# The first expert block of a transformer layer: its rows by selection products instead of a gather, bias rows added on chip, routing counts moved inside the block

## The chip, the cores and the metric

One core of a Trainium2 chip runs the whole program. Its engines are TensorE (PE, matrix products), VectorE (DVE), ScalarE (ACT), GpSimd (POOL) and SyncE (SP, whose queue only issues DMAs here). The metric is the device time of one execution in microseconds (us).

## The reference, cut to what matters

The kernel computes a whole layer: a retention branch and a differential attention branch, merged into `x_new` (512 tokens of 1024), then a mixture of 32 experts of which each token uses 4. The change touches only the passage into the experts and the first expert's block.

```python
def _moe(h, router_w, router_b, w1, b1, w2, b2):
    logits = (xt @ router_w + router_b).astype(jnp.float32)
    top_val, top_idx = lax.top_k(logits, TOP_K)          # TOP_K = 4 of N_EXPERTS = 32
    gate = jax.nn.softmax(top_val, axis=-1)
    ...                                                  # tokens sorted by expert, blocks of 128 rows
    def expert_block(args):
        xblk, e = args
        hh = xblk @ w1[e] + b1[e]
        glu = jnp.minimum(hh[:, :D_FF], SWIGLU_LIMIT)
        lin = jnp.clip(hh[:, D_FF:], -SWIGLU_LIMIT, SWIGLU_LIMIT)
        act = glu * jax.nn.sigmoid(SWIGLU_ALPHA * glu) * (lin + 1.0)
        return act @ w2[e] + b2[e]
    ...
    y = jax.ops.segment_sum(yb * row_gate[:, None], row_tok, num_segments=t + 1)[:t]
# _layer: x_new = x_new + g_f * _moe(_modulate(_rmsnorm(x_new, norm2_g), sh_f, sc_f), ...)
```

## The kernel before, in words

The order on each engine is written out by hand; semaphores tie the engines together. Each engine executes its own list in order, so an instruction that waits holds up all that stands behind it on that engine.

**Weights.** Every expert needs 12 chunks of 1 MB, eight of `exp_w1` and four of `exp_w2`. SP loads a chunk into one of six slots (`load_w1`, `load_w2`; a slot is free when DVE has used the chunk six before it, semaphore `e_lo`). ACT rounds it to a high part (`hi_e`, 1.92 us), DVE makes the low part (`lo_e`, 2.29 us), and PE multiplies three combinations (high by high, high by low, low by high), twelve matmuls of 512 columns for each chunk. Three of the six slots are not free at first: slot 3 holds rows 256 to 511 of the normalised tokens (`ht[2]`, `ht[3]`), slots 4 and 5 lie over the modulation vectors and `ht[0]`, `ht[1]`.

**Loop over experts.** `up(i)` on PE multiplies the block's 128 rows, transposed (`xthi`, `xtlo`), by the eight `exp_w1` chunks; `turn_x` transposes the rows of the next block out of the buffer that POOL's gather filled; `down(i-1)` multiplies by four `exp_w2` chunks; `turn_act(i)` transposes the activations. `item(i)` is these four in that order, 32 times (there is one extra block). Block 0 stands ahead of the loop: `up(0, bias_part)`, `turn_x`, `turn_act(0)`, and then the loop.

**Between the output projection and block 0** ("routing"). `out_part(t, c, kh)` on PE makes `x_new` of token tile t, half c. DVE adds the residual (`new_x`), ACT takes the sum of squares (`row_squares`), POOL the reciprocal root (`row_rstd`), DVE makes the rows (`scale_rows`, `shift_rows`; semaphore `n2_done`). PE transposes and multiplies by the router (`turn_rows`, `logits`; ACT copies between them, `x_columns`). DVE picks four experts (`choose(t)`, ending in the mask), PE counts places (`places(t)`), DVE computes gates and slots (`gates_of`, `place`) and, for experts 0 and 1, one-hot selection matrices (`pick_rows(t)`, tile `pick`). `first_rows(t)` multiplies those by token numbers, from which DVE makes the row lists of the first two blocks (`first_ready`). Then block 0 needs this chain: POOL gathers the 128 rows from `h2_d` in memory, SP loads the chunks 3 to 5 behind that gather, and PE does `turn_x`, ACT and DVE split the result (`x_high`, `x_low`). PE also makes counts over all tokens, flags and an item list (`route_step` 2 to 4) before block 0.

**POOL's list** writes every token's row number and gate into a table in memory (`list_tile(t)`: four indirect DMAs for each of four tiles, line 826), gathers, reads the table back (line 851), sets the next bias selector (`next_sel(0, 1)`, line 860), and adds the gated second biases into the output.

**Second bias.** PE forms gates times `b2` (`bias_part`, banks 6 and 7), ACT copies them out (`bias_out(t)`, four buffers), POOL scatter-adds each tile into `out` (line 896, four indirect DMAs of 512 KB), where SP has stored `x_new` before. Line 2089 is the helper `mm` for every matmul; lines 2504, 2605, 2616 and 2679 are transposes (of the token rows, of the gathered rows, of the activations, of the dense gates); 1231 is `hi_e`, 1913 is `lo_e`.

## Time and profile before

| | us |
|---|---|
| median of 3 runs | 2324.55 (2322.3 to 2326.19) |
| the profiled execution | 2324.45 |
| its span on the core | 2322.7 |
| PE busy in the span | 2275.3 (98%) |
| DVE busy | 1697.1 (73%) |
| ACT busy | 1222.1 (53%) |
| POOL busy | 377.7 (16%) |

The span is the time between the first and the last instruction of the core; some 2 us of the execution lie around it. A busy PE in these profiles is not PE at its peak: the granted clock (PEclk) says which of its two levels, 1.2 or 2.4 GHz, it ran at, 0.50 being 1.2 GHz. Times such as 1136.47 are microseconds from the span's start.

### The profile page before, as it was taken

The page shows a single profiled execution, that of the slowest core. Times are in us where ns is not written, and L with a number is a line of the kernel's source. Part 1 is how long each engine was busy: PE and PEld are TensorE (multiplying, and loading weights), DVE is VectorE, ACT ScalarE, POOL GpSimd, SP SyncE. Part 2 cuts the span into 40 slices and gives each one's busy share as a digit, 9 for nine tenths or more (in the row PEclk, how much of TensorE's full clock was granted, in tenths as well). Part 3 has the DMA queues.
Part 4 walks back from the last instruction along what each step waited for, and adds up shares of the span by engine and source line. Part 5 has one row for each costly group of instructions (what it writes and reads, how often), then busy time and mean ns, then how long its engine had stood idle before and what let it go on. Part 6 is the DMA issues. An engine that isn't in the chain of part 4 may idle for free.

```text
span 2322.7 us, 29938 instructions
## 1 busy us (share of the span) xinstructions
PE 2275.3 (98%) x10487; PEld 1802.7 (78%) x10487; DVE 1697.1 (73%) x1544; ACT 1222.1 (53%) x1136; POOL 377.7 (16%) x327
## 2 busy tenths in 40 slices
PE   7999999999999999999799999999999999999997
PEld 3858778686887787788678888888888888888886
DVE  4535344353636766856799999999999999999996
ACT  4212222121233723732577777777777777777774
POOL 2000000000203023000621212212211122121112
PEclk9999999999999999999799999999999999999999
DMA  8322313132231021054699999999999999999995
GB/s 294 118 91 91 127 37 128 54 123 77 73 111 52 1 91 55 1 168 161 238 378 385 370 370 379 368 375 373 374 364 371 363 370 378 367 373 376 369 372 180
DMA packets 135509, 542.89 MB, mean 234 GB/s; under 512 B 16131, under 2 KB 24467, under 8 KB 101390
## 3 DMA queue, kind: packets, MB, share of 16 engines
q1 hardware_dynamic: 123192, 516.30, 58.8%
q0 software_dynamic: 11952, 21.44, 3.8%
q10 hardware_dynamic: 296, 4.21, 0.5%
q8 instruction: 45, 0.74, 0.1%
q14 instruction: 24, 0.20, 0.0%
HBM read 533.79 MB, written 26.38 MB: 241 GB/s over the span
## 4 chain that ended last, share of the span: by engine, by line
PE 95%; DVE 1%; DMA 1%; ACT 1%; issue 0%; ACTq 0%; POOLq 0%; SPq 0%; DVEq 0%
PE ps L2089 91%; PE ps L2605 1%; PE ps L2616 1%; DMA raw<-in_w_mod 1%; PE ps L2407 1%; PE ps L2349 0%; DVE nmx L1696 0%; PE ps L2295 0%; DMA raw<-in_exp_w 0%; DMA ar<-h_d,ar 0%; ACT ar L1111 0%; PE ps L2425 0%; DVE hlo L1435 0%; PE ps L2504 0%; DVE ar L1431 0%
## 5 line engine op out<-in xcount | busy, mean ns | idle before, releaser
L2089 PE MATMUL ps<-whi,yhi 128*128 128x512 f32 x1072 | 348.5, 395 | 5.6 <-DVE yhi L2000 5.6
L2089 PE MATMUL ps<-hhi,yhi 128*128 128x512 f32 x1072 | 342.6, 389 | 0.0
L1913 DVE TENSOR_TENSOR hlo<-raw,hhi 128x2048 fp32r<-128x2048 f32 x132 | 302.4, 2292 | 48.5 <-ACT hhi L1231 48.5
L1231 ACT ACTIVATE whi<-raw 128x2048 fp32r<-128x2048 f32 x132 | 253.3, 1920 | 97.2 <-PE ps L2089 97.0
L1913 DVE TENSOR_TENSOR wlo<-raw,whi 128x2048 fp32r<-128x2048 f32 x132 | 298.8, 2284 | 4.9 <-ACT whi L1231 3.5
L1231 ACT ACTIVATE hhi<-raw 128x2048 fp32r<-128x2048 f32 x132 | 253.1, 1917 | 86.1 <-PE ps L2089 75.0
L1345 DVE TENSOR_TENSOR wlo<-raw,whi 128x2048 fp32r<-128x2048 f32 x56 | 128.2, 2289 | 219.3 <-ACT whi L929 219.3
L2089 PEld LDWEIGHTS ps<-whi,yhi 128*128 128x128 f32 x1072 | 202.6, 189 | 59.7 <-issue 12.1
L2089 PE MATMUL ps<-ar 128*128 128x128 f32 (+4 forms) x1014 | 237.5, 429 | 6.1 <-ACT ar L1145 1.4
L2089 PE MATMUL ps<-whi,hhi 128*128 128x512 f32 x592 | 233.7, 395 | 0.0
L2089 PEld LDWEIGHTS ps<-hhi,yhi 128*128 128x128 f32 x1072 | 201.2, 188 | 41.8
L2089 PE MATMUL ps<-whi,hlo 128*128 128x512 f32 x592 | 230.8, 390 | 0.0
L2089 PE MATMUL ps<-wlo,hhi 128*128 128x512 f32 x592 | 230.5, 389 | 0.0
L2089 PEld LDWEIGHTS ps<-ar 128*128 128x128 f32 (+1 forms) x1014 | 145.8, 192 | 92.5 <-issue 70.9
L929 ACT ACTIVATE whi<-raw 128x2048 fp32r<-128x2048 f32 x56 | 107.2, 1915 | 209.5 <-PE ps L2089 208.9
L2089 PE MATMUL ps<-wlo,yhi 128*128 128x512 f32 x544 | 213.1, 392 | 0.0
L2089 PE MATMUL ps<-hlo,yhi 128*128 128x512 f32 x544 | 211.7, 389 | 0.0
L2089 PE MATMUL ps<-whi,ylo 128*128 128x512 f32 x544 | 177.3, 395 | 1.9 <-DVE ylo L2019 1.9
L2089 PE MATMUL ps<-hhi,ylo 128*128 128x512 f32 x544 | 174.9, 390 | 0.6 <-DVE hlo L1913 0.5
L875 POOL DMA_INDIRECT out_x<-ar,cur x32 | 92.7, 2896 | 501.4 <-DVE ar L2029 468.8
L1913 DVE TENSOR_TENSOR wlo<-ar,whi 128x2048 fp32r<-128x2048 f32 x66 | 151.2, 2292 | 27.2 <-ACT whi L1231 27.1
L1231 ACT ACTIVATE whi<-ar 128x2048 fp32r<-128x2048 f32 x66 | 126.8, 1921 | 55.0 <-PE ps L2089 53.4
(293 smaller groups left out, 3962.8 us busy)
## 6 DMA issues: line engine op xcount, KB each, us to landing
raw<-in_exp_w SPq DMA_DIRECT2D x264, 1024.0 KB, 7.8
ar<-in_exp_w SPq DMA_DIRECT2D x132, 1024.0 KB, 7.7
raw<-in_w_in SPq DMA_DIRECT2D x44, 1024.0 KB, 5.0
raw<-in_w_mod SPq DMA_DIRECT2D x22, 1024.0 KB, 6.4
raw<-in_w_br_ret SPq DMA_DIRECT2D x8, 1024.0 KB, 5.1
ar<-in_x SPq DMA_DIRECT2D x8, 512.0 KB, 9.2
raw<-in_w_br_diff SPq DMA_DIRECT2D x4, 1024.0 KB, 5.2
raw<-in_w_out SPq DMA_DIRECT2D x4, 1024.0 KB, 10.2
```

The costliest lines, as they stand in the source:

```text
L875: pool.indirect_dma_start(a["out"], bass.IndirectOffsetOnAxis(ap=cur[:, 0:1], axis=0), F(A_Y, D), None, bounds_check=L - 1, oob_is_err=Fal ...
L929: act.activation(whi[:, j % NSPL, :, :], raw[:, s, :, :], ACT.Copy).then_inc(hi_made, 1)
L1231: act.activation(e_whi[j % ESPL], e_raw[s], ACT.Copy).then_inc(e_hi, 1)
L1345: V.tensor_tensor(wlo[:, j % NSPL, :, :], raw[:, s, :, :], whi[:, j % NSPL, :, :].bitcast(F32), ALU.subtract).then_inc(lo_made, 1)
L1913: V.tensor_tensor(e_wlo[j % ESPL], e_raw[s], e_whi[j % ESPL].bitcast(F32), ALU.subtract).then_inc(e_lo, 1)
L2089: return pe.matmul(out, lhsT, rhs, start=start, stop=stop, skip_group_check=skip)
L2407: last = pe.transpose(psf[:, TURN0 + m * P:TURN0 + (m + 1) * P], F(A_PROB, 2, 2, T)[:, u % 2, 0, m * P:(m + 1) * P], ident)
L2605: last = pe.transpose(ps[:, q, c * P:(c + 1) * P], F(A_XG, D)[:, k * P:(k + 1) * P], ident)
L2616: last = pe.transpose(ps[:, act_bank(i, hf), c * P:(c + 1) * P], F(A_AC, 2, COL)[:, hf, c * P:(c + 1) * P], ident)
```

## The change

It does the following.

1. Block 0's rows. `direct_rows(t, q)` on PE multiplies `ht[t]` by `pick[:, t, 0, :]`, 32 products of 128x128 in full precision, and so has the transposed rows of expert 0 in banks 0 and 1. The gather of block 0 goes; POOL's first gather is for expert 1, and `turn_x` for it moves into `up(0)` (after chunk 6).
2. Loads. SP loads chunk 4 as soon as the last row store is issued, chunk 5 when the stores have landed and `places(3)` is done, chunk 3 when the second `direct_rows` bank is done. None waits for a gather.
3. Routing counts, `first_rows`, flags, item list and the transposes of the gates are issued by PE after chunks 0, 1 and 2 of `up(0)` (`route(kk)`), and DVE's side of them, with `gates_of(3)` and `place(3)`, stands between `lo_e(0, 1)` and `lo_e(0, 4)`. The mask is no longer copied three times; one sum over the tiles (`mask_sums`) is.
4. The last tile's sum of squares is taken in two halves (`half_squares`), with one POOL addition more; `hi_e(0, 0)` to `hi_e(0, 2)` stand between ACT's steps of the last tile; `choose(3)` goes ahead of `shift_rows(3)`.
5. Second bias. `b2` is loaded three times, scaled by POOL (96x1024) instead of DVE, and the low part is made by POOL. `bias_part` comes one chunk later. ACT copies out into two buffers instead of four; POOL adds each tile to `x_new` on chip (`tensor_tensor` of 128x1024, `out_summed`) and stores it once. SP's four stores of `x_new` and the four scatter-adds go. `bias_out(2)` and `bias_out(3)` stand behind `glu(0)`.
6. After `up(0)` PE waits until ACT and DVE have read its banks, and starts `item(1)`; `turn_act(0)` is issued inside `up(1)`, after its chunk 1.

```diff
@@ SP
-            sp.wait_ge(first_ready, 1)
-            sp.wait_ge(gathered, 16)
-            for j in range(RSLOTS - 1, ERAW):
-                load_w1(0, 0, j)
-            for t in range(LT):
-                sp.dma_start(a["out"][t * P:(t + 1) * P, :], F(A_XN, LT, D)[:, t, :]).then_inc(stored, 16)
+            load_w1(0, 0, RSLOTS)
+            sp.wait_ge(h2_stored, 16 * LT)
+            sp.wait_ge(pos_done, LT)
+            load_w1(0, 0, RSLOTS + 1)
+            sp.wait_ge(xt_turned, 2)
+            load_w1(0, 0, RSLOTS - 1)
@@ POOL
             list_tile(1)
+            pool.wait_ge(b2_loaded, 48)
+            pool.wait_ge(vec2, 80)
+            hold()
+            pool.tensor_tensor(out=b2, in0=b2, in1=F(A_GFB, D)[0:3 * N_EXPERTS, :], op=ALU.mult).then_inc(b2_scaled, 1)
+            list_tile(2)
             pool.wait_ge(first_ready, 1)
             pool.wait_ge(h2_stored, 16 * LT)
-            gather(firsti[:, 0, 0:1])
-            list_tile(2)
+            gather(firsti[:, 1, 0:1])
+            pool.tensor_copy(cur[:, :], firsti[:, 0, :]).then_inc(cur_ready, 1)
+            pool.wait_ge(gb_hi, 1)
+            pool.tensor_tensor(out=b23[0:32, :], in0=b2[0:32, :], in1=b23[0:32, :].bitcast(F32), op=ALU.subtract).then_inc(gb_lo, 1)
             list_tile(3)
...
             next_sel(0, 1)
-            pool.wait_ge(stored, 16 * LT)
             for t in range(LT):
+                if t == LT - 1:
+                    next_gather(0, 2)
                 pool.wait_ge(gb_out, 2 * t + 2)
                 hold()
-                pool.indirect_dma_start(a["out"], bass.IndirectOffsetOnAxis(ap=lval[:, t * TOP_K, 0:1], axis=0),
...
+                pool.tensor_tensor(out=xn, in0=xn, in1=bias_rows[t % 2], op=ALU.add).then_inc(out_summed, 1)
+                pool.wait_ge(out_summed, t + 1)
+                pool.dma_start(a["out"][t * P:(t + 1) * P, :], xn).then_inc(stored, 16)
@@ ACT
             def bias_out(t):
...
+                if t >= 2:
+                    act.wait_ge(out_summed, t - 1)
...
+            for j in range(ESPL + 1, FIRST):
                 hi_e(0, j)
             bias_out(0)
+            hi_e(1, 0)
+            bias_out(1)
+            hi_e(1, 1)
+            x_high(1, (0,))
             act.activation(junk32[:, 0:1], ones[:, 0:1], ACT.Silu)
             glu(0)
+            x_high(1, (1,))
+            bias_out(2)
+            bias_out(3)
@@ DVE
             x_low(0)
+            lo_e(0, 1)
+            gates_of(3)
+            place(3)
+            dve.wait_ge(route_step, 1)
...                                      # flag, then
+            lo_e(0, 2)
+            dve.wait_ge(route_step, 2)
...                                      # lists of the first blocks, flags, then
+            lo_e(0, 3)
...                                      # bias low parts, item list, then
+            lo_e(0, 4)
@@ PE
+            def direct_rows(t, q):
+                pe.wait_ge(pick_ready, t + 1)
+                pe.wait_ge(n2_done, t + 1)
+                for c in range(4):
+                    k = 4 * q + c
+                    last = mm(ps[:, q, c * P:(c + 1) * P], ht[t][:, k * P:(k + 1) * P], pick[:, t, 0, :],
+                              t == 0 and c == 0, t == LT - 1 and c == 3, True)
+                if t == LT - 1:
+                    last.then_inc(xt_turned, 1)
...
+            pe.wait_ge(route_ready, 1)
+            direct_rows(0, 0)
             logits(3, 1)
+            direct_rows(0, 1)
+            direct_rows(1, 0)
+            direct_rows(1, 1)
             places(3)
+            for t in range(2, LT):
+                for q in range(2):
+                    direct_rows(t, q)
...
-            up(0, bias_part)
-            pe.wait_ge(gathered, 32)
-            turn_x()
-            turn_act(0)
-            pe.wait_ge(xt_lo, 4)
+            up(0, first_block)
+            pe.wait_ge(glu_done, 1)
+            pe.wait_ge(moe_step, 1)
+            pe.wait_ge(xt_lo, 3)
...
+            item(1, first_act)
```

## Rows read from the trace of the kernel before

**Rows 1.** Busy time by stage: from:to, length, then each engine's us, PEclk, DMA share, GB/s
```profile
1110.00:1120.00 10.00, 7.89 (x45) 7.12 (x43) 8.42 (x31) 3.35 (x7) 4.95 (x7) 0.76 0.20 68
1120.00:1130.00 10.00, 5.18 (x31) 4.46 (x31) 7.51 (x26) 6.55 (x6) 7.10 (x6) 0.50 0.20 46
1130.00:1140.00 10.00, 4.38 (x13) 3.26 (x12) 4.28 (x4) 6.04 (x7) 8.32 (x8) 0.50 0.97 361
1140.00:1150.00 10.00, 10.00 (x40) 8.14 (x39) 9.91 (x8) 5.76 (x3) 3.18 (x2) 0.87 1.04 394
...
1300.00:2322.00 1022.00, 1009.80 (x4687) 828.99 (x4685) 938.76 (x545) 731.43 (x484) 195.41 (x147) 1.00 0.96 361
```

**Rows 2.** The chain of waits from 1123 to 1192 us: start, us, what
```profile
1123.79 4.21 DMA ar<-h_d,ar
...
1128.12 5.09 DMA raw<-in_exp_w
...
1136.47 27.78 PE ps L2089 x108
...
1168.40 22.71 PE ps L2089 x100
```

**Rows 3.** PE in order of time: start, us, instruction, count, idle before and releaser
```profile
1137.06 0.63 PE L2089 MATMUL ps<-wlo,yhi 128*128 128x512 f32 x1
...
1138.34 0.63 PE L2089 MATMUL ps<-wlo,yhi 128*128 128x512 f32 x1
...
1143.04 0.39 PE L2089 MATMUL ps<-wlo,yhi 128*128 128x512 f32 x1
...
1143.72 0.39 PE L2089 MATMUL ps<-wlo,yhi 128*128 128x512 f32 x1
...
1166.92 1.09 PE L2616 MATMUL ps<-cst,ar 128*128 128x128 f32 x8 [1.81 <-DVE ar L2013]
```

**Rows 4.** PE in order of time, 799 us: full-precision products of 128x128, two instructions each
```profile
799.04 1.60 PE L2089 MATMUL ps<-ar 128*128 128x128 f32 x12
```

**Rows 5.** DVE in order of time, from the last tile into block 0
```profile
1113.05 0.69 DVE L1812 TENSOR_TENSOR ar<-ar,cst 128x512 f32<-128x512 f32 x1
...
1116.00 1.30 DVE L1824 SCALAR_TENSOR_TENSOR raw<-raw,rs,ar 128x1024 f32<-128x1024 f32 x1 [0.94 <-POOL rs L774]
1117.42 0.25 DVE L1842 SCALAR_TENSOR_TENSOR ar<-ps,rs,ar 128x32 f32<-128x32 f32 x1
...
1118.76 0.38 DVE L1857 TENSOR_REDUCE ar<-ar 128x32 f32<-128x128 f32 x1
...
1124.32 2.29 DVE L1913 TENSOR_TENSOR wlo<-raw,whi 128x2048 fp32r<-128x2048 f32 x1
...
1139.13 4.49 DVE L1913 TENSOR_TENSOR hlo<-raw,hhi 128x2048 fp32r<-128x2048 f32 x2
```

**Rows 6.** ACT in order of time: the first copy of the second bias out of PSUM
```profile
1150.96 1.09 ACT L1307 ACTIVATE ar<-ps 128x512 f32<-128x512 f32 x2 [1.08 <-PE ps L2089]
```

**Rows 7.** POOL in order of time, 1125 to 1154 us
```profile
1125.14 2.36 POOL L826 DMA_INDIRECT list_d<-ar  x1 [0.30 <-issue]
...
1136.06 0.96 POOL L826 DMA_INDIRECT list_d<-ar  x1 [0.30 <-issue]
...
1142.97 0.83 POOL L851 DMA_DIRECT2D ar<-list_d  x1 [0.62 <-DMA list_d<-ar]
1152.61 1.17 POOL L860 CAST hhi<-cst 128x128 fp32r<-128x128 f32 x1 [8.82 <-issue]
```

**Rows 8.** Line 851, POOL's read of the list table: issue to landing
```profile
DMA to landing us min/median/max: 8.3/8.3/8.3
```

**Rows 9.** DMA issues, 1090 to 1180 us: the load of 128 KB in the quiet stretch
```profile
ar<-in_exp_b SPq DMA_DIRECT2D x1, 128.0 KB, 3.9
```

**Rows 10.** Line 1624, a DVE product of 128x512: min, median and max ns
```profile
L1624 DVE TENSOR_TENSOR ar<-ar,rs x20: 693/1448/1454, 604.4 to 908.0; 128x512 f32<-128x512 f32 x20
```

**Rows 11.** Line 797, POOL's product of 128x512: min, median and max ns
```profile
L797 POOL TENSOR_TENSOR ar<-ar x20: 1032/1037/2082, 599.1 to 903.1; 128x512 f32<-128x512 f32 x20
```

More of the change, by code:

```diff
@@ L500, in build @@
         onehot = R(LT * TOP_K, N_EXPERTS)
-        mask3 = R(LT, 3 * N_EXPERTS)
+        mask = R(LT, N_EXPERTS)
+        mask_sums = R(3, N_EXPERTS)
         slot = R(LT * TOP_K)
@@ L1234, in _, with x_high @@
             acthi = ylo[:, 0:2, :].rearrange("p a (k n) -> p (a k) n", n=P)
-            def x_high(n):
-                for q in range(2):
+            def x_high(n, halves=(0, 1)):
+                for q in halves:
                     act.wait_ge(xt_turned, n * 2 + q + 1)
@@ L1995, in _, with x_low @@
             actlo = ylo[:, 2:4, :].rearrange("p a (k n) -> p (a k) n", n=P)
-            def x_low(n):
-                for q in range(2):
+            def x_low(n, halves=(0, 1)):
+                for q in halves:
                     dve.wait_ge(xt_hi, n * 2 + q + 1)
@@ L2045, in _ @@
             x_low(0)
-            for j in range(1, KH):
-                lo_e(0, j)
+            lo_e(0, 1)
+            gates_of(3)
+            place(3)
+            dve.wait_ge(route_step, 1)
+            V.tensor_scalar(small[0:96, 0:1], ps[0:96, 0, 0:1], cst[0:96, C_THR:C_THR + 1], None,
+                            ALU.is_gt).then_inc(flag_ready, 1)
+            lo_e(0, 2)
+            dve.wait_ge(route_step, 2)
+            firsti = first[:, :, :].bitcast(I32)
+            tl.did(V.tensor_scalar(pad[:, 2:4], ps[:, 1, 0:8:4], pad[:, 1:2], pad[:, 0:1], ALU.mult, ALU.add))
+            tl.did(V.tensor_copy(first[:, 0, 1:2], ps[:, 1, 2:3]))
+            tl.did(V.tensor_copy(first[:, 1, 1:2], ps[:, 1, 7:8]))
+            tl.wait()
+            V.tensor_tensor(firsti[:, :, 0:1], pad[:, 2:4].unsqueeze(2), ps[:, 1, 1:8:4].unsqueeze(2),
+                            ALU.add).then_inc(first_ready, 1)
+            dve.wait_ge(route_step, 3)
+            tl.did(V.tensor_copy(small[0:96, 1:2], ps[0:96, 0, 0:1]))
+            tl.wait()
+            dve.wait_ge(flag_ready, 1)
+            V.tensor_scalar(small[0:96, 8:8 + OVER + 2], iota[0:96, 0:OVER + 2], small[0:96, 1:2], small[0:96, 0:1],
+                            ALU.is_equal, ALU.mult).then_inc(flag_ready, 1)
+            lo_e(0, 3)
             dve.wait_ge(ones_made, 5)
@@ L2609, in turn_act @@
                 pe.wait_ge(act_done, i + 1)
-                if isinstance(i, int):
+                early = isinstance(i, int) and i == 0
+                if early:
                     pe.wait_ge(gb_out, 2 * LT)
                 for hf in range(2):
-                    if not isinstance(i, int):
+                    if not early:
                         pe.wait_ge(xt_lo, i * 2 + 3 + hf)
@@ L2622, in up @@
                 pe.wait_ge(e_lo, chunk(i, 0) + 1)
-                late = isinstance(i, int)
+                late = isinstance(i, int) and i == 0
                 def add_bias():
@@ L2666, in down, with item @@
                     last.then_inc(e_used, 1)
-            def item(i):
-                up(i)
-                pe.wait_ge(gathered, i * 16 + 32)
+            def item(i, between=None):
+                up(i, between)
+                pe.wait_ge(gathered, i * 16 + 16)
                 pe.wait_ge(act_lo, i * 2)
@@ L2674, in item, with first_block @@
                 turn_act(i)
-            pe.wait_ge(route_ready, LT)
-            pe.wait_ge(dense_ready, LT)
-            for t in range(LT):
-                last = pe.transpose(ps[0:N_EXPERTS, 7, t * P:(t + 1) * P], dense[:, t, 2:2 + N_EXPERTS], ident)
-            last.then_inc(route_step, 1)
-            pe.wait_ge(first_ready, 1)
-            pe.wait_ge(items_ready, 1)
-            pe.wait_ge(gathered, 16)
-            turn_x()
-            pe.wait_ge(xt_lo, 1)
-            def bias_part(kk):
-                t = kk - 3
+            pe.wait_ge(route_ready, LT - 1)
+            pe.wait_ge(xt_lo, 1)
+            def first_block(kk):
+                if kk < 3:
+                    route(kk)
+                if kk == FIRST - 2:
+                    pe.wait_ge(items_ready, 1)
+                    pe.wait_ge(first_ready, 1)
+                    pe.wait_ge(gathered, 16)
+                    turn_x()
+                t = kk - 4
                 if not 0 <= t < LT:
```

198 lines of the change are left out of this document (90 added, 108 removed).

## The prediction, made before the changed kernel was seen to run

> **What bounds the kernel now.** I read the busy time by stage first. From 1300 us to the end PE is busy 1009.8 of 1022 us at full clock, DVE 939 and the DMA engines 0.96 [rows 1]: in the expert loop PE is the bound, and nothing that the change does there shortens it. The hole is ahead of it: from 1110 to 1140 PE works 17.5 us of 30 and the granted clock falls to 0.50, the 1.2 GHz level, where it stays until past 1140. Then the chain of waits through the hole: the gather of block 0's rows takes 4.21 us, the load of chunk 3 that stands behind it 5.09 us, and PE starts block 0 at 1136.47; it has done `up(0)` at 1164.25 and starts the loop at 1168.40 [rows 2]. After that the chain is PE alone, 35.3 us for each block. So the change is worth what it moves the point at which PE gets through `up(1)`, less the work that it puts on PE on the way. The third view is each engine in order of time, since the new order has to be followed.
>
> **Start of block 0.** `new_x` of the last half tile ended at 1113.74 [rows 5]; without two mask copies and with `scale_rows` ahead of `choose(2)` it ends some 0.6 us sooner. The halved squares save about 0.4 us and the added POOL addition, one more small step there, costs back about 0.3 (all three are estimates). `choose(3)` no longer stands behind `shift_rows(3)`: it starts when its logits are there, about 1115.7 instead of 1117.42, and its mask takes 1.7 us as now (1117.42 to 1119.14) [rows 5], 1117.5. Then the sum over the mask, `shift_rows(3)` (1.3) [rows 5] and `pick_rows(3)` (0.7): the last selection matrix stands at 1119.9. PE has 32 selection products; twelve instructions, that is six products of this size, took 1.60 us including one drain of 0.28 [rows 4], so 0.24 to 0.27 each, taken as 0.25; 28 of them lie behind the last logits, 7.0 us, with 0.4 for `places(3)`: the last bank is done at 1122.9, the first 1.0 earlier. One copy on ACT (0.57) and one subtraction on DVE (0.7) give block 0 its start at 1123.3, against 1136.47: 13.2 us. This is the mechanism that the change is built on, and I believe it. These products keep PE working in full array passes where it idled, so I take the clock as full here; were it at 1.2 GHz, the 28 products would take twice as long, 7 us more.
>
> **Inside block 0.** Chunks cost PE 12 matmuls of 0.227 us (0.68 for three) at full clock and 0.427 at half (1.28 for three) [rows 3]. In block 0 about 14 ran at half clock, so `up(0)` at full clock is 27.78 - 14 x 0.2 = 24.9 us. The change adds `route(0)` to `route(2)`, some 26 small products and four transposes at 0.11 us per instruction, 3.2 us, and `turn_x` of 0.9 us. It also adds waits, since DVE gives only 2.21 us per low part (4.49 for two) [rows 5] and now does `gates_of(3)` and `place(3)` (2.3 us), lists and flags (1.3), bias low parts (1.4) and the item list (0.8) between them. Walking DVE through: `lo_e(0, 2)` ends at 1132.3 where PE wants it at 1130.9 (1.4 us), `lo_e(0, 4)` at 1141.9 where PE wants it at 1139.1 (2.9 us, of which 2.0 are POOL's, below). With these the last product of `up(0)` is at 1156.1, before it was 1164.25: 8.1 of the 13.2 us are left.
>
> **POOL and DVE exclude one another.** POOL's product of 128x512 takes 1.03 us [rows 11]. The DVE product at line 1624 takes 0.69 us alone and 1.45 when POOL's falls on it [rows 10]. The other way round, an indirect DMA issue of POOL takes 0.96 us beside an idle DVE and 2.36 at 1125.14, when the low part of 1124.32 ran; it ended 0.9 us after that [rows 5, 7]; the selector copy at 1152.61 took 1.17 for 0.29 in the same way. So where DVE makes low parts back to back, POOL gets one issue done for each of them, 2.2 us instead of 0.96 + 0.30. And the 96x1024 and 128x1024 operations that move to POOL (six of them) are priced at 2 x 1.03 = 2.07 us each for POOL and at up to as much for DVE. The Trainium skill (SBUF - State Buffer, "SBUF: two separate sides") says that this port pair is an exclusive lock, held for the whole instruction, and that a DVE operation with two SBUF inputs takes it too. By that rule each of the four additions costs DVE its full 2.07 us; the row at line 1624 shows 0.76 of 1.03 lost, by which it would be 1.5.
>
> **What is late next: POOL's list.** In the new order the loop cannot start before POOL has (a) read the list back and made the selector of block 1 (`next_sel(0, 1)`), and (b) added tile 0, because `bias_part(3)` on PE waits for `bias_out(2)`, and that for `out_summed` 1. Queued behind that wait are, on ACT, `hi_e(1, 2)` and all later high parts, on PE the whole loop. Before, line 860 ran at 1152.61 [rows 7], 16 us ahead of the loop. POOL's list of work, each step at its own duration and held by DVE as above: `list_tile(1)` ends at 1123.1; scaling `b2` 2.07, 1125.2; `list_tile(2)` among `lo_e(0, 1)` to `lo_e(0, 3)`, 1134.5; gather and `cur` 1137.5; low part of `b2` 2.07, 1139.6; `list_tile(3)` among `lo_e(0, 4)` to `lo_e(0, 7)`, four issues at 2.2 to 3.0 us, 1150.3 (1141.8 if DVE never holds it). Then the table writes land: 3.2 us after the issue, as the gather's 4.21 less its 1.05 of issue [rows 2] (5.9 us in the full queues before, from 1137.0 to 1142.9). The read-back of 128 KB took 8.3 us in full queues [rows 8]; a load of that size in a quiet stretch took 3.9 [rows 9]. The queues are fuller than quiet and emptier than before (SP's 2 MB of stores at 1129 to 1132, with loads issued right behind them, are gone, but loads still follow each low part), so I take 4.3: 1157.8. Register loads and the selector 1.3, as from 1151.3 to 1152.6; the addition 2.07, 1161.3; `bias_out(2)` 1.09 [rows 6]; `bias_part(3)` 0.5. The loop starts at 1163, before at 1168.40. That is 5.4 us.
> The Trainium skill (SBUF - State Buffer, "The DMA setup-cost knee") gives a fixed cost of about 2 us for any transfer; taken for both landings this is an estimate of 1159.7 for the loop's start and of 2320 for the time. The landings above are longer wherever the trace has one.
>
> **Behind the start.** PE has then stood for over 6 us. In the trace it came out of such a stretch at half clock for 6 us, 14 matmuls at 0.2 us more [rows 1, 3]: 2.9 us. `turn_act(0)`, 0.87 us, is now inside `up(1)`. Its old wait for the activation (1.81 us) [rows 3] is gone, and that is in the start already. The other POOL additions fall on DVE's low parts of block 1, but PE at half clock leaves DVE room: nothing. The loads hide: chunk 4 is issued at 1119 where the first was at 1128.1, and chunk 3, issued at 1123, has landed by 1130, ahead of `hi_e(0, 3)`'s use. The end of the kernel stays as it is.
>
> **The sum.** 5.4 - 0.9 - 2.9 = 1.6 us off the profiled execution of 2324.45, which stands 0.1 us from the median: 2323.0.
>
> **The rivals.** (1) *The list is on time.* If POOL's issues slip in between DVE's operations, `list_tile(3)` ends at 1142 to 1145, and the additions are ahead of need. Then the loop starts 3.3 us behind `up(0)` (`glu(0)` 1.0, `x_high` 0.55, `bias_out(2)` 1.1, `bias_part(3)` 0.5): 1159.4, 9.0 us early. Less 0.9 for `turn_act(0)`, and less 1.4 for a low part of block 1 that an addition delays: 6.7 us, 2317.8. No clock is lost. For it: many issues in the trace did take 0.96. Against it: those fell where DVE idled. (2) *Slower: the list is later still.* If landings are as in the trace of before (5.9 and 8.3 us) and the addition waits for one low part (2.2), the loop starts at 1172, 3.6 us late; with 0.9 and 2.9 on top 7.4 us slower: 2331.9. Place: line 851's landing. The price turns into a loss once the loop starts later than 1164.6. For it: those are the only durations that the trace has of these two transfers. Against it: the queues had just been given 2 MB of stores then. (3) *Block 0 starts late*, at half clock (7 us more) or because `shift_rows(3)` comes after `choose(3)`. POOL's list hides most of this: some 3 us more than the forecast, 2326. That the gather leaves the chain is not in doubt; a variant in which the change gives nothing for lack of effect has no chance of its own.
>
> **How the numbers follow.** The forecast 0.45 (2320 to 2326), rival 1 0.30 (2314 to 2320), rival 2 0.17 (2328 to 2334), rival 3 0.08. A measurement can tell about 0.2% here, 4.65 us: faster means below 2319.9, slower above 2329.2. Faster takes rival 1 and a little of the forecast's edge, 0.34; slower most of rival 2 and a little of rival 3, 0.18; within, 0.48. The range leaves out the far half of rival 2 and the far edge of rival 1: 2315.5 to 2330.5. The likeliest case alone has 2320 to 2326.
>
> **What would show it.** In the profile after: PE's first 512-column matmul of block 0 near 1123 (right) or past 1127 (the selection products or the clock); clock 1.00 from 1110 to 1155; line 1913's low part 4 ending near 1142; POOL's `list_tile(3)` issues near 2.2 us each and ending near 1150 (rival 1: 1.3 and 1144); the read-back landing near 1158; the loop's start near 1163 with PE idle 6 us ahead of it and at half clock behind it. Wrong is the prediction if PE is not idle there (rival 1), or if the loop starts past 1165 (rival 2).

## The result and the profile after

The kernel after takes 2326.91 us in the median (2323.67 to 2330.49), the kernel before 2323.42 beside it (2321.79 to 2326.19): ratio 1.0014, 95% interval [1.0008, 1.0021]. It is 3.5 us slower, where 1.6 us faster was forecast; the time lies inside the range. The profiled execution took 2326.59 us with a span of 2324.8.

The same stages as in [rows 1], then the chain of waits as in [rows 2] (start, us, what) and PE's own waits (us in total, times, longest):

```profile
1110.00:1120.00 10.00, 8.47 (x74) 8.17 (x73) 8.08 (x22) 6.02 (x10) 6.40 (x9) 1.00 0.30 97
1120.00:1130.00 10.00, 8.22 (x37) 7.39 (x37) 8.29 (x10) 2.14 (x3) 8.86 (x5) 0.66 0.91 311
1130.00:1140.00 10.00, 10.00 (x59) 8.20 (x59) 9.21 (x22) 5.85 (x5) 4.42 (x2) 1.00 0.98 353
1140.00:1150.00 10.00, 8.87 (x39) 6.41 (x38) 9.94 (x5) 8.08 (x8) 9.22 (x5) 1.00 0.80 288
1150.00:1160.00 10.00, 6.20 (x32) 4.86 (x30) 6.54 (x7) 5.88 (x7) 3.76 (x3) 0.91 0.84 322
1160.00:1170.00 10.00, 3.40 (x9) 1.92 (x10) 1.80 (x1) 2.36 (x5) 6.59 (x6) 0.50 0.49 172
```
```profile
1135.57 3.90 POOL ar L835
1139.49 1.77 POOL cur L855
1141.26 2.38 POOL ylo L858
...
1151.34 7.09 DMA list_d<-ar
1158.43 0.29 issue
1158.71 2.67 DMA ar<-list_d
...
1163.06 2.31 POOL ar L908
1165.41 0.04 issue
1165.46 1.09 ACT ar L1325 x2
1166.55 0.04 issue
1166.60 9.46 PE ps L2098 x30
```
```profile
PE ps L2098 <- ACT ar L1325: 10.4, 1, 10.4
PE ps L2098 <- DVE ar L1911: 3.1, 1, 3.1
PE ps L2098 <- DVE wlo L1931: 1.1, 2, 0.7
```

The hole of [rows 1] at 1110 to 1140 is gone: PE works 26.7 of 30 us there. It has moved to 1150 to 1170, where PE works 9.6 of 20 us; from 1160 on the granted clock is at 0.50, the 1.2 GHz level. The second view names what ends last there: POOL's list of work (gather, `cur`, low part of `b2`, `list_tile(3)`), the landing of the list, its read-back, the first addition, `bias_out(2)`. That is the chain of the forecast. In the third view PE waits 10.4 us for `bias_out(2)` and 3.1 us for `pick_rows(3)`.

The profiles differ ahead of the change as well, so times of the passage are counted from an anchor that all kernels share, the start of the eight transposes of `turn_rows(1)` (1091.27 before, 1089.53 after). From the end of `up(1)` to the last transposes of the loop every profile has 1106.1 us, so a kernel's span is the sum of the anchor, the column "`up(1)` done", 1106.1 and the last column. The columns between are start times counted from the anchor. E-numbers are the experiments; e5, e10 to e13 and e15 are told in the text.

| kernel | anchor | block 0 starts | last product of `up(0)` | loop starts | `up(1)` done | last transposes to the end |
|---|---|---|---|---|---|---|
| before | 1091.27 | 45.20 | 72.57 | 77.13 | 99.68 | 25.68 |
| after | 1089.53 | 35.79 | 66.28 | 78.21 | 103.58 | 25.60 |
| after, second profile (e9) | 1089.57 | 31.54 | 66.11 | 76.77 | 102.86 | 28.38 |
| e1 | 1090.47 | 31.54 | 66.85 | 70.48 | 96.40 | 28.26 |
| e2 | 1091.02 | 31.54 | 67.05 | 72.16 | 99.04 | 26.98 |
| e3 | 1090.97 | 31.54 | 65.88 | 76.71 | 101.96 | 27.28 |
| e4 | 1089.38 | 31.54 | 66.48 | 73.21 | 99.61 | 28.14 |
| e6 | 1089.68 | 31.54 | 66.03 | 72.43 | 97.31 | 26.94 |
| e7 | 1089.47 | 31.54 | 70.68 | 74.31 | 99.00 | 26.96 |
| e8 | 1090.85 | 31.54 | 62.14 | 65.99 | 95.07 | 26.91 |
| e16 | 1089.74 | 31.54 | 67.65 | 71.77 | 98.08 | 25.60 |
| e17 | 1089.75 | 31.54 | 66.80 | 75.29 | 101.64 | 25.63 |
| e14 | 1089.13 | 31.54 | 63.68 | 67.48 | 96.53 | 25.97 |
| e18 | 1089.55 | 31.54 | 62.10 | 65.73 | 91.63 | 25.95 |

Block 0 starts 9.4 us sooner than before, the last product of `up(0)` comes 6.3 sooner, and the loop starts 1.1 us later; `up(1)` is done 3.9 us later. The anchor gave 1.7 back in this profile, so the span is 2.1 longer.

In this profile one more thing shows: DVE and POOL collide. The rows are DVE with `pick_rows(3)` at line 1911, then POOL with a list issue at line 831 and the scaling of `b2` at line 849, then PE before and behind its wait:

```profile
1118.39 3.33 DVE L1911 TENSOR_SCALAR ar<-ar 128x128 f32<-128x128 f32 x2
```
```profile
1118.30 0.96 POOL L831 DMA_INDIRECT list_d<-ar  x1 [0.30 <-issue]
1119.29 2.35 POOL L849 TENSOR_TENSOR ar<-ar 96x1024 f32<-96x1024 f32 x1
1121.81 2.99 POOL L831 DMA_INDIRECT list_d<-ar  x1 [0.17 <-issue]
...
1135.57 3.90 POOL L835 DMA_INDIRECT ar<-h_d,ar  x1 [5.62 <-DVE ar L2042]
```
```profile
1116.69 2.03 PE L2098 MATMUL ps<-ar,raw 128*128 128x128 f32 x16
1121.78 3.78 PE L2098 MATMUL ps<-ar,raw 128*128 128x128 f32 x16 [3.06 <-DVE ar L1911]
```

`pick_rows(3)` takes 0.48 us in every other profile of these kernels and 3.33 here: it ends at 1121.72, when POOL has ended both the issue and the scaling (1121.64). It also began 1.1 us later from the anchor than in e9, behind a wait for PE of 1.03 us whose reason stays open. PE stands 3.06 us, falls to the lower level, and makes the last 16 products in 3.78 us instead of 2.03 (at full clock 0.13 each, as in [rows 4]). Less the 0.57 us that PE stands ahead of block 0 in e9, this is the difference between 31.54 and 35.79 in the table.

### The profile page after: what moved, and what is told of

Same layout as the page of the kernel before. It is cut to its first block, busy times and chain, and to the rows that moved or that the text cites. A ratio compares the mean times of both kernels' runs of the same rounds, so it can differ in the third digit from the quotient of the medians.

```text
span 2324.8 us, 30027 instructions
## 1 busy us (share of the span) xinstructions
PE 2278.1 (98%) x10537; PEld 1805.2 (78%) x10537; DVE 1698.8 (73%) x1535; ACT 1221.6 (53%) x1137; POOL 370.8 (16%) x333
## 4 chain that ended last, share of the span: by engine, by line
PE 95%; DVE 1%; POOL 1%; DMA 1%; ACT 1%; issue 1%; POOLq 0%; DVEq 0%; SPq 0%; ACTq 0%
PE ps L2098 91%; PE ps L2651 1%; PE ps L2639 1%; PE ps L2416 1%; PE ps L2358 0%; DMA raw<-in_w_mod 0%; DMA list_d<-ar 0%; DVE nmx L1713 0%; PE ps L2304 0%; POOL list_d L831 0%; ACT ar L956 0%; POOL ar L835 0%; PE ps L2513 0%; ACT ar L1122 0%; PE ps L2434 0%
## 5 line engine op out<-in xcount | busy, mean ns | idle before, releaser
L2098 PE MATMUL ps<-ar 128*128 128x128 f32 (+5 forms) x1046 | 239.0, 422 | 3.0 <-ACT ar L1156 1.4
L885 POOL DMA_INDIRECT out_x<-ar,cur x32 | 86.5, 2704 | 508.7 <-DVE ar L2012 476.0
L1931 DVE TENSOR_TENSOR hlo<-ar,hhi 128x2048 fp32r<-128x2048 f32 x66 | 148.3, 2287 | 10.8 <-ACT hhi L1248 10.8
```

The costliest lines, as they stand in the source:

```text
L885: pool.indirect_dma_start(a["out"], bass.IndirectOffsetOnAxis(ap=cur[:, 0:1], axis=0), F(A_Y, D), None, bounds_check=L - 1, oob_is_err=Fal ...
L1931: V.tensor_tensor(e_wlo[j % ESPL], e_raw[s], e_whi[j % ESPL].bitcast(F32), ALU.subtract).then_inc(e_lo, 1)
L2098: return pe.matmul(out, lhsT, rhs, start=start, stop=stop, skip_group_check=skip)
```

## The experiments

Medians stand beside those of the kernel before on the same chip.

**Who holds the loop's start.** e1 moves POOL's additions of tiles 0 and 1, with `next_sel(0, 1)`, ahead of the wait for the list; e2 only the selector; e3 puts four powers of 128x8 (7.45 us on POOL, results unused) behind `list_tile(3)`; e4 puts the scaling of `b2` behind `list_tile(2)`.

```diff
# e1
+            next_sel(0, 1)
+            for t in range(2):
+                add_tile(t)
             pool.wait_ge(listed, 16 * LT * TOP_K)
...
-            next_sel(0, 1)
-            for t in range(LT):
+            for t in range(2, LT):
# e3
             list_tile(3)
+            for k in range(4):
+                hold()
+                pool.tensor_tensor(out=idle_t[:, 8 * k:8 * k + 8], in0=ones[:, 0:8], in1=ones[:, 8:16], op=ALU.pow)
```

> The changed kernel with POOL's order altered: the selector of block 1 and the additions of tiles 0 and 1 stand ahead of the wait for the list and of its read-back. Theory (POOL's list and read-back hold up the loop, through bias_out(2) and bias_part(3)): PE's stand of 10.4 us ahead of the last bias_part shrinks to about 3 us, the loop starts some 7.5 us sooner, and if the clock then holds another 2 us come back: ratio to the kernel before 0.998 (about 2319; 2317 with the clock), against 1.0014 for the changed kernel. Rival (DVE, held by POOL's operations, is what is late in block 0 and block 1): the additions only move DVE's losses elsewhere, ratio stays within 0.001 of 1.0014.

> The changed kernel with only the selector of block 1 ahead of the wait for the list; the additions stay behind the read-back. Theory: no change in time (ratio 1.0014 within 0.0007), PE's stand stays near 10 us, since the addition of tile 0 is the later of the two. If the selector alone were what the loop waits for, the time would fall by up to 4 us.

> The changed kernel with four small POOL operations (128x8 powers, 2.08 us each in the trace of before) put behind list_tile(3); they write a scratch tile that nobody reads. Theory: POOL's list is on the path, so the whole delay, some 8 us, or about 5 where it runs while the list writes are landing (5.5 us between the last write and the read-back), shows: the wait for the landing covers up to 5.5 us of it, so 3 to 8 us slower than the changed kernel. Rival (POOL is off the path): no change.

> The changed kernel with POOL's scaling of b2 moved behind list_tile(2), so that it doesn't fall on DVE's pick_rows(3). Theory: pick_rows(3) takes 0.5 us instead of 3.3, PE doesn't stand 3.1 us ahead of the last selection products and the clock doesn't fall there (1.8 us), block 0 starts 4 us sooner, first_ready comes 2 to 4 us sooner, and with it POOL's list and the loop: 2 to 4 us faster than the changed kernel, ratio 0.9997 to 1.0006. Rival (POOL's list is late for its own length and not for first_ready): no change in time, though block 0 starts sooner.

Before 2323.67. e1 2322.32, ratio 0.9991 [0.9982, 1.0]; e2 2325.84, 1.0010 [1.0001, 1.0019]; e3 2328.31, 1.0016 [1.0007, 1.0025]; e4 2324.86, 1.0005 [0.9996, 1.0014]. PE's waits in e1:

```profile
PE ps L2103 <- DVE wlo L1936: 4.9, 3, 3.1
PE ps L2103 <- ACT ar L1330: 2.6, 1, 2.6
PE ps L2103 <- DVE hlo L1936: 2.1, 2, 1.4
```

With two additions ahead of the wait for the list the wait for `bias_out(2)` falls from 10.4 to 2.6 us (9.1 in e9, the second profile of the kernel after) and the loop starts at 70.5: the addition behind the list is the link. The time fell by 4.6 us and not by the nearly 8 expected; PE now waits 7.0 us for low parts, where it is 4.4 in e9.

e2's median stayed where it was expected, but its profile did not: PE waits 4.1 us for `bias_out(2)`, not near 10, and the loop starts 4.6 us sooner than in e9. The addition is still behind the read-back. About 2 us of the difference are in the addition, which took 2.34 us in e2 and 4.37 in e9, beside a low part of DVE. The medians of the two (2325.84 and 2325.69) do not show it at all, so e2 does not settle what the selector alone costs.

e3 was expected 3 to 8 us slower than the kernel after; its ratio is the same within the intervals (1.0016 and 1.0014). In the profile its 7.45 us moved the loop by nothing against e9 (76.71 and 76.77): 4.7 of them fell into the time in which POOL had waited for the list's landing anyway, and the rest was made up in the read-back (3.8 us to the selector in e3, 5.5 in e9) and in the addition (2.33 us in e3, 4.37 in e9). So this experiment does not price a delay of POOL; it shows the landing's wait as slack for POOL, not for the chain.

e4 takes the scaling out of the way of `pick_rows(3)`. It holds `hi_e(0, 3)`, which stands on ACT behind the copy of the scaled rows (it started after 10.51 us of waiting), and PE waits 5.0 us there, so `up(0)` ends no sooner than in e9. But POOL's list ended 3.0 us sooner than in e9 and the loop started 3.6 sooner. The ratio is within the range that was expected.

**The same delay in the kernel before, and parts undone.** e5 is the kernel before with e3's four powers. e6 is the kernel after with the scatter-adds, SP's stores of `x_new` and the four bias buffers back. e7 is the kernel after with `list_tile(3)` ahead of the wait for `first_ready`.

```diff
# e6
+            for t in range(LT):
+                sp.dma_start(a["out"][t * P:(t + 1) * P, :], F(A_XN, LT, D)[:, t, :]).then_inc(stored, 16)
...
-                pool.tensor_tensor(out=xn, in0=xn, in1=bias_rows[t % 2], op=ALU.add).then_inc(out_summed, 1)
...
+                pool.indirect_dma_start(a["out"], bass.IndirectOffsetOnAxis(ap=lval[:, t * TOP_K, 0:1], axis=0),
# e7
             list_tile(2)
+            list_tile(3)
             pool.wait_ge(first_ready, 1)
```

> The kernel before with the same four small powers on POOL behind `list_tile(3)`, 7.45 us of POOL time, that the kernel after was given. Theory (POOL's list became the last link only through the change): in the trace of before line 860 ran 16 us ahead of the loop, so 7.45 us vanish in that slack: 2323.4, within 1 us of the kernel before, and PE's row of waits as in [rows 2]. Rival (any 7 us of POOL work in this stretch cost, through DVE or through the loop's own POOL steps): 2326 or more.

> The kernel after with its selection products and routing inside block 0, but with the second-bias rows stored as before: four stores of x by SP, four scatter-adds by POOL, four bias buffers. `bias_out(2)` then waits for no addition. Theory (the wait of `bias_out(2)` for POOL's addition is what held the loop's start): the loop starts 3 to 5 us behind the last product of `up(0)`, 71 to 73 us after the anchor where it was at 78.2; with the 2 MB of stores in the queues some 1 to 2 us go back to late chunks: 2320 to 2323. Rival (the start and the clock of block 0 are what cost): still 2326 to 2327.

> The kernel after with `list_tile(3)` ahead of POOL's wait for `first_ready` (the gather of block 1's rows, `cur` and the low part of `b2` come behind it). Theory (POOL stood 5.6 us idle in the middle of its list and that time is on the path): the list's writes, the read-back and the first addition come 4 to 5 us sooner, the loop starts at 73 to 75 after the anchor, time 2323 to 2324.5. Rival 1 (the idle time is hidden, since the list's landing is paced by DVE's low parts): 2326 to 2327. Rival 2 (the gather for block 1 now becomes late for `turn_x`): PE shows a wait for the gathered rows inside block 0 of 2 us or more, and the time is 2326 or above.

Before 2323.52. e5 2324.39, 1.0001 [0.9992, 1.001]: in the kernel before the list is off the path; the powers took 10.46 us there, held by DVE, and cost nothing that can be measured. e6 2323.76, 1.0002 [0.9993, 1.0011]: the loop starts at 72.4 instead of 76.8 to 78.2, and 2 to 3 us come back in the median (against 2325.69 of e9 and 2326.91). That is a little short of the 2320 to 2323 expected: without the additions on chip the change is even with the kernel before, not faster. e7 2324.58, 1.0003 [0.9994, 1.0012], with both of its mechanisms at once:

```profile
PE ps L2098 <- POOL ylo L859: 6.1, 1, 6.1
PE ps L2098 <- ACT ar L1325: 2.6, 1, 2.6
```

The wait for `bias_out(2)` is down to 2.6 us, so the end of `list_tile(3)` was on the path. It does not show that the 5.62 us were, in which POOL stood idle in the first profile: without the collision they are gone from the kernel after too (in e9 POOL stands 0.30 us ahead of its gather). What e7 takes out from ahead of `list_tile(3)` is the gather, `cur` and the low part of `b2`, 5.8 us in e9. And now PE waits 6.1 us inside block 0, not for the gathered rows, as the second rival had it, but for POOL's low part of `b2`, which stands behind the same four issues.

**Improving on it.** e8 is e1 with chunk 3 loaded ahead of chunk 5 and with both products of the second bias on DVE; e16 has the first of the two alone (in the diff, what follows the loads is e8's, on DVE; the two POOL products go).

```diff
             sp.wait_ge(pos_done, LT)
-            load_w1(0, 0, RSLOTS + 1)
             sp.wait_ge(xt_turned, 2)
             load_w1(0, 0, RSLOTS - 1)
+            load_w1(0, 0, RSLOTS + 1)
...
             lo_e(0, 1)
...
+            V.tensor_tensor(b2, b2, F(A_GFB, D)[0:3 * N_EXPERTS, :], ALU.mult).then_inc(b2_scaled, 1)
...
             lo_e(0, 3)
...
+            V.tensor_tensor(b23[0:32, :], b2[0:32, :], b23[0:32, :].bitcast(F32), ALU.subtract).then_inc(gb_lo, 1)
```

> The order of the additions of e1 (two tiles ahead of the wait for the list), and two further moves: SP issues chunk 3's load ahead of chunk 5's, and the two products of the second bias (scaling and low part) are made by DVE, 1.22 us each, behind `lo_e(0, 1)` and `lo_e(0, 3)`, and no longer by POOL at 2.4 us each with DVE held. Theory (in e1 PE's 4.9 us of waits inside block 0 come from chunk 3's late landing and from POOL's product lying on DVE's bias rows): those waits fall to 2 to 3 us, 2319.5 to 2320.5. Rival (the waits inside block 0 are absorbed by the waits ahead of the loop): 2322.3 as e1.

> e1 with chunk 3's load issued ahead of chunk 5's and nothing else; the two products of the second bias stay on POOL. Theory (both parts of e8 carry: chunk 3's landing, and POOL's products lying on DVE): half of the 2.7 us between e1 and e8, 2320.5 to 2321.5. Rival 1 (the landing is all): 2319.7. Rival 2 (POOL's products are all): 2322.3.

e8: 2319.65 beside 2323.52, 0.9975 [0.9964, 0.9986]. e16: 2322.43 beside 2323.93, 0.9995 [0.9985, 1.0004], no better than e1 (0.9991). The landing alone brings nothing, since the next wait takes its place; PE's first row of waits in e16:

```profile
PE ps L2103 <- POOL ylo L858: 3.8, 1, 3.8
```

POOL's low part took 2.4 us plus what DVE held it; on DVE it took 1.21, and `bias_lo` beside it 1.40 instead of the 3.56 that e1 had. The last product of `up(0)` comes at 62.1 instead of 66.9. e16's median is that of its second rival, but no run has the DVE products without the load, so how the 2.7 us between e1 and e8 divide stays open.

**The end of the kernel.** In most profiles of kernels with the changed PE program the last column of the table is 1.2 to 2.7 us longer. From the last transposes to the first product of the last `down` (kernel before, kernel after, e9):

```profile
2297.02 1.03 PE L2616 MATMUL ps<-cst,ar 128*128 128x128 f32 x8
2299.95 0.49 PE L2089 MATMUL ps<-whi,ylo 128*128 128x512 f32 x1 [1.90 <-DVE ylo L2019]
```
```profile
2299.20 1.03 PE L2651 MATMUL ps<-cst,ar 128*128 128x128 f32 x8
2303.21 0.49 PE L2098 MATMUL ps<-whi,ylo 128*128 128x512 f32 x1 [2.98 <-issue]
```
```profile
2298.52 1.03 PE L2651 MATMUL ps<-cst,ar 128*128 128x128 f32 x8
2302.75 0.79 PE L2098 MATMUL ps<-whi,ylo 128*128 128x512 f32 x1 [3.19 <-issue]
```

Before, PE waits until DVE has the operand, 2.93 us in all (2.98 in e5, with the same PE program). After, it stands 4.01 and 4.23 us and the profile shows nothing that it waits for ("issue"); between the two lie only the jumps past the blocks that are not needed. In e9 the clock then falls, which it did not in the first profile (columns as in [rows 1]):

```profile
2300.52:2302.52 2.00, 0.00 (x0) 0.00 (x0) 1.02 (x3) 2.00 (x2) 1.59 (x1) 0.84 0.04 8
2302.52:2304.52 2.00, 1.77 (x4) 1.49 (x5) 2.00 (x2) 1.31 (x1) 0.00 (x0) 0.50 0.42 41
2304.52:2306.52 2.00, 2.00 (x6) 1.52 (x6) 2.00 (x1) 0.00 (x0) 0.00 (x0) 0.50 0.36 70
```

In the first profile of the kernel after the longer stand cost nothing. In the kernel before PE waits once more inside this `down`, for the low part of its last chunk; in the kernel after it comes there later and finds it made. The chains of waits, before and after:

```profile
2302.91 2.30 DVE hlo L1913
2305.21 0.04 issue
2305.25 7.11 PE ps L2089 x30
```
```profile
2301.91 1.30 issue
2303.21 11.34 PE ps L2098 x48
```

From the last transposes to the end of these products are 15.34 and 15.35 us. In e9, with the clock down behind the stand, they are 18.19.

e9 is the kernel after unchanged. e10, e11 and e12 are e8 with 64, 128 and 192 more PE instructions (waits that always hold) in the part that is jumped over. e13 is the kernel before with 200 more of them at the start of its PE program, as many as the change added; e14 and e15 are e8 with 56 and 128 more at the start. The diff is e14's; two such waits make one instruction.

```diff
             pe.wait_ge(c_made, 3)
+            for _ in range(112):
+                pe.wait_ge(s_cvec, 48)
```

> The kernel after, unchanged, profiled a second time. In its first profile POOL's scaling of `b2` lay on `pick_rows(3)` (3.33 us for two instructions of 0.48) and block 0 started 35.8 us after the anchor; in the four profiles of e1 to e4, whose programs are the same up to that point or one step later, it started at 31.5. Theory A (the collision is the rule of this program): again 35 to 36, the loop at 77 to 79. Theory B (it is a race that falls either way): 31.5, the loop at 74 to 76, and the profiled time 1.5 to 3 us shorter. The median stays at 2326 to 2327 in either.

> e8 with 64 more PE instructions (waits that always hold) in the part of the program for a 36th block and later, which is jumped over here. No engine does anything more. In the end of the profile PE stood 2.9 to 3.2 us with no wait to explain it ahead of its last `down` in every kernel with the changed PE program, and 1.9 us, ended by a wait for DVE, in the two with the old one. Theory A (where the code behind the jump lies decides when PE gets it): the stand changes by 1 us or more for one of the three sizes, and the granted clock stays at 1.00 behind it there: 2317 to 2318.5. Rival (the stand belongs to the jump itself or to data): the same 3.9 us from the last transposes to the first product in all three, 2319.65 as e8.

> As e10, with 128 instructions. Theory A: the interval from the last transposes to the first product of `down` differs from e8's 3.90 us in at least one of the three. Rival: 3.9 us and 2319.65.

> As e10, with 192 instructions. Theory A: the interval from the last transposes to the first product of `down` differs from e8's 3.90 us in at least one of the three. Rival: 3.9 us and 2319.65.

> The kernel before with 200 more PE instructions (waits that always hold) at the start of PE's program, where PE waits for the first loads anyway; the change had added 200 to it. Theory B (the length of PE's program ahead of the loop decides how fast PE gets through the jumps behind the loop): the interval from the last transposes to the first product of the last `down` grows from 2.93 to about 3.9 us, in part of the runs the granted clock falls to 0.50 behind it, and the time is 1 to 2 us longer, 2324.5 to 2325.5. Rival (what precedes the jump, not where it lies, makes the difference): 2.93 us and 2323.5.

> e8 with 56 more PE instructions at the start of PE's program (256 more than before in all). Theory B: the interval at the end goes from e8's 3.90 us back to about 2.9, the clock stays at 1.00 there, time 2317 to 2318.5. Rival: 3.9 us and 2320.

> e8 with 128 more PE instructions at the start of PE's program. Theory B: an interval that differs from e8's 3.90 us by 0.5 us or more in this run or in e14. Rival: 3.9 us and 2320.

e9: `pick_rows(3)` took 0.48 and block 0 started at 31.54, so the collision of the first profile is a race that can fall either way (theory B). But `up(1)` was done only 0.7 us sooner, since POOL's list and the addition took the rest: the profiled time was not shorter but 2.2 us longer, 2328.77, with 2.8 us more at the end than in the first profile. Its median was 2325.69, 1.001 [1.0, 1.002].

e10 to e12: 2320.04, 2320.17, 2320.77 beside 2323.58; the interval from the last transposes to the first product is 3.92, 4.29, 4.22 us against e8's 3.90. Moving the code behind the jump does nothing of use. Lengthening it at the front does: in e13 the kernel before has an interval of 4.46 us, again without a cause in the profile.

```profile
PE ps L2089 <- issue: 3.4, 1, 3.4
```

Its median, 2340.79 beside 2323.93, is no measure of that, and here the expectation was wrong by far: the 200 instructions were not hidden. PE's first products of the modulation start at 25.43 us instead of 9.64. In e15 they start at 17.48, and its 2326.41 is spoiled in the same way; in e14 at 9.69, which is no delay. Both e14 and e15 have the interval back at 2.93 us, with the same cause as before:

```profile
2291.73 1.04 PE L2656 MATMUL ps<-cst,ar 128*128 128x128 f32 x8
2294.66 0.49 PE L2101 MATMUL ps<-whi,ylo 128*128 128x512 f32 x1 [1.90 <-DVE ylo L2000]
```

So with 0, 256 and 328 instructions more than before at the front the interval is 2.93 to 3.05, with 200 it is 3.9 to 4.5. With 200 the clock fell behind the stand in 12 of 14 profiles and the last column was 1.2 to 2.7 us longer; in the other two, the first of the kernel after and e16, it did not fall, and the column is 25.60 as before. With the other lengths the column is 25.6 to 26.0 in all six profiles, even in e18, where the clock fell there as well (0.69 over 4 us). Which lengths are good, and what PE does in that time, stays open: four lengths are too few for a rule.

e14 took 2317.11 beside 2323.93, 0.9964 [0.995, 0.9978], in only five runs. e17 is the kernel after with the 56 instructions and nothing else, e18 is e14 again.

> The kernel after with 56 more PE instructions (waits that always hold) at the start of PE's program and nothing else. Theory B (the place of PE's loop in its program costs the change 1.0 to 2.8 us at its end): the interval from the last transposes to the first product of the last `down` is 2.93 us where it was 4.0 and 4.2 in the two profiles of the kernel after, the granted clock stays at 1.00 behind it, and the median falls by 1 to 2 us to 2324 to 2325.5; what is left over the kernel before is the late loop start. Rival (the end is short again, but the median does not follow, since PE's end is hidden behind the last scatter-add's landing): 2325.7 to 2327.

> e14 unchanged, for a closer value: the additions of two tiles ahead of the list, chunk 3 ahead of chunk 5, the two products of the second bias on DVE, 56 PE instructions at the start. Theory: 2317 to 2318, 2 us below e8. Rival (e14's value came from few runs): 2319.5.

Before 2323.41. e17: 2323.33, 1.0001 [0.9992, 1.001]. Fifty-six instructions that do nothing took 3.6 us off the first median of the kernel after, 2.4 off that of e9, more than the 1 to 2 expected; the interval was 3.05 us and the clock 1.00. By the profiles the end gives 0 to 2.8 us of that; that its loop also started 1.5 us ahead of e9's, and 2.9 ahead of the first profile's, is within what these kernels vary by. So the instructions undo the loss in the median, and the end is the place where the profiles show them to act; how much of the 3.6 us it gave is not shown. e18: 2317.45, 0.9974 [0.9964, 0.9985]. This version beats the kernel before by 6 us and the kernel after by 9.

## Why the prediction was wrong, point by point

The step that failed is the term "5.4 us" of the sum, the earlier start of the loop: the chain from POOL's list through its landing and read-back to the first addition was taken too short, and the loop started 1.1 us later than before in the first profile and only 0.4 sooner in e9. The second is "the end of the kernel stays as it is".

**What bounds the kernel.** Right: 1106.1 us of loop in every profile, whatever stood ahead of it.

**Start of block 0.** Forecast 13.2 us sooner; 9.4 in the first profile, 13.7 in all others of the table (45.20 to 31.54). The sum was right; missing was the race of POOL's issue and scaling with `pick_rows(3)`, worth 4.3 us when it falls badly. The prediction had priced POOL's moved operations at up to 2.07 us for DVE each, but had looked for their victims among the low parts, not at the one step for which PE was waiting. The price of a selection product was right, 0.24 us at full clock (32 instructions, two for each product, in 3.82 us in e9), though [rows 4], less the drain, give 0.22.

**Inside block 0.** The last product was forecast 8.1 us sooner and came 6.3 and 6.5 sooner. The terms as given add up to 1156.6, not 1156.1, so to 7.6. The list of waits was incomplete: chunk 3 landed at 1129.8 in e9 and at 1131.5 in e1, and `hi_e(0, 3)` waited 5.47 and 6.28 us for it. That "the loads hide" was wrong; but e16, with that load first, was no faster than e1, since POOL's low part of `b2` came next.

**POOL and DVE exclude one another.** Right in kind, and the sizes were low. POOL's 128x1024 addition was taken at 2.07 us and takes 2.33 to 2.43 alone, up to 4.37 behind a low part; its list issues beside low parts ran 1.8 to 3.2 us (2.2 to 3.0 forecast). The Trainium skill (SBUF - State Buffer, "SBUF: two separate sides") calls the pair an exclusive lock held for the whole instruction. `pick_rows(3)` agrees: it became 2.85 us longer beside an issue of 0.96 and a scaling of 2.35 and ended with them, so it lost more than the 0.76 of 1.03 that the row at line 1624 had lost.

**POOL's list.** Right as to the chain; this is the term that was mis-sized. Counted from the anchor, `list_tile(3)` ended at 63.7 (59.0 forecast): 5.62 us of idleness for `first_ready`, which the collision had made late, a gather issue of 3.90 and a low part of `b2` of 2.40 lay ahead of it. The landing took 5.5 us instead of 3.2; the read-back 2.7 instead of 4.3 (8.3 in [rows 8]); from there to the loop 6.4 instead of 5.2, with `bias_part(3)` at half clock. The loop started 1.1 us late instead of 5.4 early. In e9, without the collision, the list ended at 58.9, as forecast, but the loop started only 0.4 us early: the landing took 4.7, the read-back 4.2, registers and selector 2.2 instead of 1.3, and the addition 4.37 instead of 2.07, beside a low part. So the list's own length was right but for the race, and what is behind it was too short. The Trainium skill's fixed cost of some 2 us for a transfer (SBUF - State Buffer, "The DMA setup-cost knee") was too low for both: the list's landing took 4.5 to 5.5 us, and the read-back 2.7 to 6.3 (e4).

**Behind the start.** 0.9 for `turn_act(0)` and 2.9 for the clock were forecast; measured, `up(1)` lost 2.8 us between the loop's start and its end (1.1 to 3.9) in the first profile and 3.5 in e9. Right.

**The end.** "The end of the kernel stays as it is" is the second step that failed, and it was not even among the rivals. It cost nothing in the first profile and 2.7 us in the second, and with 56 instructions more the median was that of the kernel before (e17). How the measured 3.5 us divide between the loop's start and the end stays open; each of e1, e6 and e17 brings the median back to about that of the kernel before.

**The sum.** That the time lies inside the range says little for the forecast, since the range reached from 9 us faster to 6 slower. For the profiled execution: 3.9 late at `up(1)`, less 1.7 at the anchor, 0.1 at the end, 2.1 us longer against 2324.45, as measured; the 1.7 at the anchor were luck. Of the rivals, the late list came nearest: it was given 2331.9 with the loop at 1172, and was said to turn into a loss past 1164.6. From the anchor of before, the loop came at 1169.5.

**What had to show.** PE's first product of block 0 near 1123 came at 1125.32 in the first profile, in e9 at 1121.11. The clock of 1.00 from 1110 to 1155 was wrong (0.66 in 1120 to 1130), and so was `list_tile(3)` near 1150 (1153.2). PE's idleness ahead of the loop was there, 10.4 us instead of 6.

## What to carry to other kernels

When the engine that bounds is given an earlier start, look for what now ends last, and put nothing there that collides with a step that anybody waits for; work moved from DVE to POOL was charged twice, once on POOL and once on DVE. An addition that frees a buffer belongs ahead of a wait for a transfer, not behind it (e1). And a change that adds instructions to the bounding engine can move a few microseconds at a jump far away: compare the end of the profile too, and test with instructions that do nothing before the change itself is blamed. Finally, profile a kernel twice before a place in its profile is explained: the collision here was in one profile and in no other.

## What the runs showed of the hardware

The length of PE's program ahead of its loop changes how long PE stands at the jumps behind it: 2.93 to 3.05 us, or 3.9 to 4.5 us (e13 to e15, e17).

At the start of PE's program 200 instructions that hold 400 satisfied waits took it nearly 16 us (25.43 against 9.64), 128 instructions took 8, and 56 took nothing visible behind the wait for the first load.

The same stand of PE does not always cost the clock. e14 and e18 are one program with nearly the same waits of PE, and from 1153 us on they differ so (first e14, then e18, columns as in [rows 1]):

```profile
1153.00:1163.00 10.00, 7.42 (x26) 5.10 (x26) 8.62 (x6) 7.17 (x8) 3.14 (x3) 0.83 0.70 258
1163.00:1173.00 10.00, 7.67 (x38) 6.09 (x37) 9.78 (x5) 8.18 (x6) 7.17 (x6) 1.00 0.87 306
1173.00:1183.00 10.00, 9.90 (x37) 8.08 (x38) 9.57 (x5) 3.94 (x3) 0.60 (x1) 0.83 0.91 338
```
```profile
1153.00:1163.00 10.00, 8.38 (x41) 6.50 (x42) 9.01 (x6) 7.06 (x10) 4.48 (x4) 1.00 0.76 261
1163.00:1173.00 10.00, 8.22 (x36) 6.10 (x35) 10.00 (x6) 8.92 (x6) 7.19 (x5) 1.00 0.98 358
1173.00:1183.00 10.00, 10.00 (x49) 8.33 (x50) 10.00 (x5) 5.96 (x5) 0.94 (x2) 1.00 0.95 356
```

In these rows the clock of e14 is down twice and that of e18 not at all; `up(1)` was done 4.9 us apart (96.53 and 91.63). The 19 runs of the kernel after are ordered in the same way: the mean granted clock over the whole run is 0.997 in the quickest (2323.67) and 0.992 in the slowest (2330.49). The anchor goes with the clock too. Leaving out e13 and e15, in seven profiles, the one of before among them, the clock was 0.83 in the mean of 50 to 60 us and the anchor came at 1090.8 to 1091.4; in the others it was 1.00 and the anchor at 1089.1 to 1089.8, but for e1 (1090.47). The row of before:

```profile
50.00:60.00 10.00, 10.00 (x42) 8.19 (x41) 8.77 (x18) 6.72 (x9) 1.40 (x1) 0.83 0.51 195
```

So programs that are the same up to there can differ by 1.5 us far from any change (e11 has 1.00 and an anchor of 1089.60, e10 and e12 have 0.83, 1091.08 and 1090.96), and two profiles of one kernel by 2.8 at the end: places are to be compared from an anchor, and kernels by medians. Whether the program before falls at 50 us more often than the program after can't be told from its two profiles.
